# A hybrid recurrent decoder step: dense units moved into the sample steps, masks made a pair ahead, and the RWKV sample steps and norm reordered

## What is computed

```
h = x + 0.5 * swiglu(rmsnorm(x), w_ff1)
P = rmsnorm(h) @ w_in            # one projection: gated DeltaNet, GLA, RWKV-7 and three branch gates
y_A = gated_delta(conv(P_A), state_gdn)      # 6 heads, 128 x 128 state
y_B = gla(P_B, state_gla)                    # 6 heads, 64 x 128 state
y_C = rwkv7(shift(P_C), state_rwkv)          # 12 heads, 64 x 64 state; group norm, bonus, gate
m = sum_i sigmoid(P_gate_i) * (y_i @ w_branch[i]);  h = h + m @ w_out
x = rmsnorm(h + 0.5 * swiglu(rmsnorm(h), w_ff2))
```

## Time and profile before

| | us |
|---|---|
| median of 3 runs (lowest to highest) | 3218.73 (3212.09 to 3221.67) |
| the profiled execution's own time | 3215.23 |
| its span, first to last instruction | 3213.4 |
| PE busy in the span | 3080.0 (96%) |
| DVE, ACT, POOL busy | 1671.0, 1182.4, 109.9 |
| mean granted TensorE clock | 0.974 of full speed |

### The profile page before, as it was taken

The page is one execution under the profiler, slowest core; times in us unless marked ns, Lnnn a source line. Parts: engine busy times, 40 slices in busy tenths (PEclk is TensorE's granted clock), DMA queues, the critical chain, the costliest instruction groups (busy, mean ns, idle before and its releaser), DMA issues.

```text
span 3213.4 us, 61472 instructions
## 1 busy us (share of the span) xinstructions
PE 3080.0 (96%) x24976; PEld 2966.6 (92%) x24976; DVE 1671.0 (52%) x2174; ACT 1182.4 (37%) x1589; POOL 109.9 (3%) x176
## 2 busy tenths in 40 slices
PE   8999999999899999999889998997999999999998
PEld 7999999999899888888888988886999999999998
DVE  5455445454545665555575546456455444445543
ACT  4343333333434532222253224344343333333333
POOL 1000000001000000000000001011000000000001
PEclk9999999999999999998989989989999999999999
DMA  5555555655455533334553336357545655555553
GB/s 166 166 157 169 172 157 164 171 161 171 124 170 149 152 109 95 90 105 117 166 148 95 101 115 184 108 175 252 165 131 161 170 165 170 158 169 157 167 170 112
DMA packets 599915, 482.51 MB, mean 150 GB/s; under 512 B 29010, under 2 KB 545597, under 8 KB 599389
## 3 DMA queue, kind: packets, MB, share of 16 engines
q1 hardware_dynamic: 575760, 428.45, 45.7%
q0 software_dynamic: 8592, 33.16, 3.4%
q10 hardware_dynamic: 15392, 18.43, 1.6%
HBM read 451.82 MB, written 28.10 MB: 149 GB/s over the span
## 4 chain that ended last, share of the span: by engine, by line
PE 85%; DVE 7%; ACT 3%; issue 2%; DMA 2%; ACTq 0%; POOL 0%; DVEq 0%; POOLq 0%
PE ps L392 25%; PE ps L393 24%; PE ps L394 24%; PE ps L1111 2%; DVE lo L749 2%; ACT hi L559 1%; PE ps L1106 1%; PE ps L1392 0%; DMA smA<-in_dt_bias 0%; PE ps L551 0%; PE ps L2308 0%; PE ps L1405 0%; DMA rawsD<-kept 0%; PE ps L1935 0%; DVE raws L773 0%
## 5 line engine op out<-in xcount | busy, mean ns | idle before, releaser
L392 PE MATMUL ps<-xh,hi 128*128 128x288 f32 x4800 | 1456.4, 303 | 45.7 <-ACT kept L630 11.2
L393 PE MATMUL ps<-xl,hi 128*128 128x288 f32 x4800 | 1430.0, 298 | 0.0
L394 PE MATMUL ps<-xh,lo 128*128 128x288 f32 x4800 | 1429.1, 298 | 0.0
L749 DVE TENSOR_TENSOR lo<-raw,hi 128x1024 fp32r<-128x1024 f32 (+1 forms) x820 | 975.1, 1213 | 542.8 <-ACT hi L559 533.2
L559 ACT ACTIVATE hi<-raw 128x1024 fp32r<-128x1024 f32 (+1 forms) x820 | 832.5, 1042 | 843.3 <-PE ps L394 797.6
L392 PEld LDWEIGHTS ps<-xh,hi 128*128 128x128 f32 x4800 | 915.9, 191 | 77.8 <-issue 25.1
L393 PEld LDWEIGHTS ps<-xl,hi 128*128 128x128 f32 x4800 | 916.2, 191 | 0.6
L394 PEld LDWEIGHTS ps<-xh,lo 128*128 128x128 f32 x4800 | 915.8, 191 | 0.0
L393 PE MATMUL ps<-hidl,hi 128*128 128x288 f32 x1376 | 406.9, 296 | 0.0
L392 PE MATMUL ps<-hidh,hi 128*128 128x288 f32 x1376 | 406.9, 296 | 0.0
L394 PE MATMUL ps<-hidh,lo 128*128 128x288 f32 x1376 | 404.3, 294 | 0.0
(11 more groups left out here) (680 smaller groups left out, 2022.0 us busy)
## 6 DMA issues: line engine op xcount, KB each, us to landing
raw<-in_w_ff_up SPq DMA_DIRECT2D x688, 256.0 KB, 4.1
raw<-in_w_in SPq DMA_DIRECT2D x448, 256.0 KB, 3.0
raw<-in_w_ff_down SPq DMA_DIRECT2D x344, 256.0 KB, 3.4
raw<-in_w_out SPq DMA_DIRECT2D x64, 256.0 KB, 3.0
raw<-in_w_branch SPq DMA_DIRECT2D x48, 256.0 KB, 3.0
gatesD<-kept ACTq DMA_DIRECT2D x24, 288.0 KB, 3.0
gates<-gatesD POOLq DMA_DIRECT2D x8, 864.0 KB, 7.2
raw<-in_w_branch SPq DMA_DIRECT2D x48, 128.0 KB, 3.4
```

What stands on the lines that cost most here:

```text
L392: pe.matmul(out, w, rh, start=start, stop=False)
L393: pe.matmul(out, w, rl, start=False, stop=False)
L394: return pe.matmul(out, wl, rh, start=False, stop=stop)
L749: dve.tensor_tensor(lo[:, q, 0:wide], raw[:, q, 0:wide], hi[:, q, 0:wide].bitcast(F32), SUB).then_inc(lo_ready[q], 1)
```

## The change

The number of dense units in all is the same. What changes:

- The table `U`: one unit more in each sample step of RWKV (`ssz`) and A (`asso`), four more in those of GLA (`bsso`), one more behind GLA's chunk steps (`bsco`), fewer before RWKV's norm (`rec`, `fin2`) and more behind it (`fin4`). Behind GLA's head norm 210 dense matmuls stood before; now there are 126.
- RWKV's sample steps: two buffers `sdC`, loaded two pairs ahead; PE transposes the next pair's states right behind the product with 8 columns of this pair; DVE copies only the 64x64 blocks, back into the buffer; the mask is made one pair ahead. The next load now waits until the pair's new states are copied (`C_so8`).
- RWKV's norm: the bonus products are made first, into `rsF`; mean, variance and bonus sums follow one another; gain, bonus, shift and gate are fused into 12 instructions of 288 columns.
- A's start: `rowsA` and `smA` are loaded before `mixer_done`, and `projA` as soon as PE has read `proj` the last time; 36 small copies become 2; ACT copies the old rows out later.
- The waits for the stored prompt state: in A moved down, in B gone (POOL alone waits, between its two loads). GLA's masks are made one pair ahead, and a `presplit(2)` is added in GLA's start.
- In `branch` ACT makes the high half of `merged` one slot later, behind the next split; `out` no longer waits for all groups before it to be read.

```diff
-                if not (down or name.startswith("up") and name != "up00" and name != "up10"):
+                if not (down or name == "out" or name.startswith("up") and name != "up00" and name != "up10"):
                     pe.wait_ge(acc_empty, p["group0"])
...
+            def merged_high(k):
+                act.wait_ge(sem("gated"), k + 1)
+                pair = slice(2 * k, 2 * k + 2)
+                act.activation(xh[:, pair, :], merged[:, pair, :], ACT.Copy).then_inc(sem("merged_hi"), 1)
...
+                            if s % 2 == 0 and it * 4 + s // 2:
+                                merged_high(it * 4 + s // 2 - 1)
...
-                        if name == "branch":
-
-                            act.wait_ge(sem("gated"), it * 4 + (g + 1))
-                            pair = bass.ds((it * 4 + g) * 2, 2)
-                            act.activation(xh[:, pair, :], merged[:, pair, :], ACT.Copy).then_inc(sem("merged_hi"), 1)
+                        if name == "branch" and it * 4 + g == KD // 2 - 1:
+                            merged_high(it * 4 + g)
...
-        U = dict(feat=6, hist=12, shift=60, rec=6, root=3, bfeat=8, lora=6, lora2=3, kk=8, prod=7, tok=2,
-                 wz=2, z=1, scz=1, sco=2, s0t=2, ssz=2, szt=2, sso=3, s8t=2, fin=4,
-                 conv=3, head=8, hl=8, aba=4, gc=6, aprod=7, az=4, ascz=2, asco=6, assz=2, asso=3,
-                 bgk=20, fin2=15, hn=8, afin=6, afin2=8, bfin=2, bfin2=16, bprod=4, bsco=6, bsso=4)
+        U = dict(feat=6, hist=12, shift=60, rec=2, root=3, bfeat=8, lora=6, lora2=3, kk=8, prod=7, tok=2,
+                 wz=2, z=1, scz=1, sco=2, s0t=2, ssz=3, szt=2, sso=3, s8t=2, fin=5,
+                 conv=3, head=8, hl=8, aba=4, gc=6, aprod=7, az=4, ascz=2, asco=6, assz=2, asso=4,
+                 bgk=20, fin2=2, fin3=3, fin4=8, hn=8, afin=6, afin2=8, bfin=2, bfin2=16, bprod=4, bsco=7, bsso=8)
...
+            load_sd(1)
             for p in range(BT):
-                e.need("C_sd_used")
-                if p < BT - 1:
-                    load_sd(p + 1)
                 e.need("C_so8")
+                if p < BT - 2:
+                    load_sd(p + 2)
                 for par in range(2):
                     pool.dma_start(o["rwkv_s"][0, :, 2 * p + par].rearrange("b v k -> v b k"),
...
+                        state_turned(p0)
                         for p in range(3):
-                            e.eng.wait_ge(sem("C_sd"), 32 * (p0 + p + 1))
-                            for k in range(NSEQ):
-                                mm = pe.transpose(ps[:, k // 4, k % 4 * P:k % 4 * P + P], t["sd"][:, k, :], ident[:, :])
-                            e.mark(mm, "C_s0t")
-                            weave(U["s0t"])
...
                             e.mark(mm, "ss_z")
+                            if p < 2:
+                                state_turned(p0 + p + 1)
+                            weave(U["s0t"])
                             e.need("ss_v_kept")
+                            if p:
+                                e.need("C_so8")
                             for k in range(2):
                                 out = ps[:, k, :].rearrange("p (b v) -> p b v", v=P)
                                 pe.matmul(out, t["klT"][0:32, p, :], t["vm"][:, 4 * k:4 * k + 4, :], start=True, stop=False)
...
-                            e.need("C_so8")
+                        e.need("C_so8")
 
             weave(U["rec"])
-            e.need("C_recurred")
             for p in range(BT):
                 mm = pe.matmul(ps[:, p, 0:NT], ones64[:, :], ybuf[:, YC + p, :], start=True, stop=True)
...
-            e.need("hn_sq")
+            e.need("hn_sq", 2)
...
-            e.need("hn_sq")
+            e.need("sums_read", 2)
             for p in range(BT):
-                mm = pe.matmul(ps[:, p, 0:NT], ones64[:, :], sqF[:, p, :], start=True, stop=True)
+                mm = pe.matmul(ps[:, p, 0:NT], ones64[:, :], rsF[:, p, :], start=True, stop=True)
             e.mark(mm, "hn_sum")
-            weave(U["fin"])
+            weave(U["fin3"])
...
-            weave(U["fin"])
+            weave(U["fin4"])
...
+                        state_kept(p0)
+                        masked_v(0)
                         for p in range(3):
-                            e.need("C_s0t")
-                            e.mark(dve.tensor_copy(t["s0"][:, :, :], psf[:, 0:1024].rearrange("p (b v) -> p b v", v=P)), "C_s0_kept")
...
+                            if p < 2:
+                                masked_v(p + 1)
...
             for p in range(BT):
-                e.link(dve.tensor_scalar(Y[:, p, :], Y[:, p, :], par1[:, R_LNW + p:R_LNW + p + 1], par1[:, R_LNB + p:R_LNB + p + 1], MUL, ADD))
-                ins = dve.scalar_tensor_tensor(sqF[:, p, :], proj[:, p, 0:NT], par1[:, R_RK + p:R_RK + p + 1], proj[:, 6 + p, 0:NT], MUL, MUL)
+                ins = dve.scalar_tensor_tensor(rsF[:, p, :], proj[:, p, 0:NT], par1[:, R_RK + p:R_RK + p + 1], proj[:, 6 + p, 0:NT], MUL, MUL)
...
+            weave(U["rec"])
+            e.need("hn_sum", 2)
+            e.link(dve.scalar_tensor_tensor(Y, PS6, -1.0 / 64, Y, MUL, ADD))
+            e.mark(dve.tensor_tensor(sqF[:, :, :], Y, Y, MUL), "hn_sq")
+            dve.wait_ge(sem("C_so8_stored"), 6)
+            dve.nop().then_inc(sem("C_recurred"), 1)
             weave(U["fin"])
+            weave.presplit(2)
...
+            e.mark(dve.tensor_tensor(rsF[:, :, :], PS6, proj[:, 12:18, 0:NT], MUL), "gn_bonus_used")
+            weave(U["fin2"])
+            e.need("fin_rs")
+            e.link(dve.tensor_tensor(Y, Y, sqF[:, :, :], MUL))
+            for p in range(BT):
+                e.link(dve.scalar_tensor_tensor(Y[:, p, :], Y[:, p, :], par1[:, R_LNW + p:R_LNW + p + 1], rsF[:, p, :], MUL, ADD))
+            weave(U["fin3"])
             e.need("hn_sum")
-            e.link(dve.tensor_tensor(Y, PS6, Y, MUL))
+            for p in range(BT):
+                e.link(dve.scalar_tensor_tensor(Y[:, p, :], Y[:, p, :], par1[:, R_LNB + p:R_LNB + p + 1], ps[:, p, 0:NT], ADD, MUL))
+            weave(U["fin4"])
             dve.nop().then_inc(sem("mixer_done"), 1)
...
-            pool.wait_ge(sem("mixer_done"), 1)
             pool.dma_start(rowsA[0:24, :], i["state_gdn_conv"][0].rearrange("b j n -> (b j) n")).then_inc(sem("a_landed"), 16)
+            for k, name in ((0, "a_log"), (1, "dt_bias")):
+                pool.dma_start(smA[:, k, :], i[name][0].partition_broadcast(P)).then_inc(sem("a_landed"), 16)
             pool.wait_ge(sem("kept_stored"), 16 * GROUPS_A)
+            e.need("hn_sum", 5)
             for k in range(4):
                 pool.dma_start(proj[:, 6 * k:6 * k + 6, :], projA[:, 6 * k:6 * k + 6, :]).then_inc(sem("projA_landed"), 16)
...
-            for k, name in ((0, "a_log"), (1, "dt_bias")):
-                pool.dma_start(smA[:, k, :], i[name][0].partition_broadcast(P)).then_inc(sem("a_landed"), 16)
+            state_in = lambda h: i["state_gdn"][0, :, h].rearrange("b k v -> k b v")
+            pool.wait_ge(sem("mixer_done"), 1)
+            load_state(pool, tA[1], 0, "A", state_in, 3)
+            load_state(pool, tA[1], 1, "A", state_in, 3)
...
+            load_state(pool, tA[1], 2, "A", state_in, 3)
...
+            pe.wait_ge(sem("mixer_done"), 1)
...
-            e.need("last_turned")
-            e.mark(act.activation(rowsA[0:27, :], psf[0:27, 512:512 + 2304], ACT.Copy), "rows_kept")
+            e.link(act.activation(spare, ones[:, 0:1], ACT.Silu))
+            e.need("last_kept", 2)
...
+                if m == 1:
+                    e.need("last_turned")
+                    e.mark(act.activation(rowsA[0:27, :], psf[0:27, 512:512 + 2304], ACT.Copy), "rows_kept")
...
+            tails = proj[:, 0:18, SEQW:PW].rearrange("p m (b t) -> p m b t", t=7)
+            e.link(dve.tensor_copy(tails[:, :, :, 0:GAP], ps[:, 0, 0:432].rearrange("p (m b t) -> p m b t", b=NSEQ, t=GAP)))
...
+            e.mark(dve.tensor_copy(lastA[:, :, GAP:27].rearrange("p m (b t) -> p m b t", t=GAP), tails[:, :, :, TS:]), "last_kept")
...
-                    dve.wait_ge(sem("state_stored"), 1)
...
+                if b == 2:
+                    dve.wait_ge(sem("state_stored"), 1)
...
+            load_state(pool, tB[1], 0, "B", state_in, 2)
             pool.wait_ge(sem("out_stored"), 16 * stored)
-            pool.nop().then_inc(sem("state_stored"), 2)
...
+            load_state(pool, tB[1], 1, "B", state_in, 2)
...
+            weave.presplit(2)
...
-                    dve.wait_ge(sem("state_stored"), 2)
...
+                    masked_v(0)
+                    for p in range(3):
...
+                        if p < 2:
+                            masked_v(p + 1)
```

109 lines of the change are left out of this document (52 added, 57 removed).

## The result

| | us |
|---|---|
| after: median of 5 runs (lowest to highest) | 3194.04 (3188.97 to 3200.81) |
| before, beside it on the same chip: median of 5 | 3221.67 (3212.09 to 3228.76) |
| ratio, 95% interval | 0.9911 (0.9889 to 0.9933) |
| the profiled execution of after: own time, span, clock | 3200.81, 3199.0, 0.972 |

The account below looks back on a forecast made before the run. PE is busy 96% of the span, so only its idle time and clock loss can be won; terms sum to 60, less 4 for `kept`, 56 us under the profiled 3215.2, giving 3159, predicted as 3161 us (3148 to 3177).

Parts of the forecast that it names:

- RWKV's sample steps: 0: RWKV's sample steps: idle won 2.2 us, new waits cost 7.6, clock gains 5; sum 0, between -6 and +8.
- two new waits: RWKV's sample steps: PE waits for DVE's state copy, 2.8 us in all, and for the late load, 4.8.
- its clock's term: RWKV's sample steps: a third of the 13.8 us lost to the lower clock comes back, 5 us.
- A's start: Start of A, 1593 to 1640 us: wait for `smA` goes, idle and clock loss shrink; gain 17 us, 8 to 21.
- the 4 for `kept`: PE's waits for `kept` in five places, 9.3 us: groups' ends shift, so 4 us is set against them.
- A's sample steps with GLA's start: A's sample steps gain 5 us by a unit more per step; GLA's start gains 4 by the added presplit.
- branch and out: End of the mixers: branch gains 8.5 us as DVE's wait for ACT's split goes; out gains 4.5, half its loss.
- some 5 where a new wait falls in: RWKV's sample steps: us without a dense unit where a new wait falls, against 4.2 before and 2.7 in other steps.
- RWKV's norm: RWKV's norm, 1550 to 1593 us: bonus products first and fused instructions under dense units gain 5 of 5.8 us.
- A's and GLA's third blocks: Third blocks of A and GLA: the wait behind POOL's store of the prompt state goes, gaining 6.5 and 5.5 us.
- GLA's sample steps: GLA's sample steps, clock 0.61: four more units win back a third of 12.1 us lost, 4 us, 0 to 9.
- the early load starves the weights: Rival, chance 0.2: loading `projA` crowds out weights, A's start gains 9 us, branch 0 to 2; 3177 to 3185 us.

Follow-up runs that it names:

- rwkv_steps_as_before: The kernel after with RWKV's sample steps alone in their old form, dense units per step as in after: 3173.66 us, 0.9857 of before.
- Group 5: Best version of the study (paced gate loads, 49 units moved) with RWKV's steps as in after, 3179.85 us, with either of two edits, or with both, 3164.99 us.
- turned_behind_mask_product: After, with RWKV's next transposes behind the mask's product and its three units, and two units ahead of each half's first product: 3173.94 us, 0.9862; again 3171.39, 0.9869.
- group 5's single edits: RWKV's order of after plus two dense units in each half's first pair, 3172.90 us, or plus transposes moved behind the mask's product, 3172.65 us.
- a_start_as_before: turned_behind_mask_product with A's start alone in its old form (load order, 36 small copies, early copy of old rows): 3184.61 us, 0.9906 of before.
- no_late_loads: After without the loads of RWKV's sample states for pairs 2 to 5, which then work on old data: 3175.67 us, 0.9866 of before.
- the base: turned_behind_mask_product run again unchanged, beside the kernels of the third group: 3171.39 us, 0.9869 of before.
- gates_paced: turned_behind_mask_product with POOL asking for a pair's gates and raws in branch three pairs ahead instead of four: 3169.36 us, 0.9847 of before.

## Why the prediction was wrong

The direction was right, and the gain came to half of the sum: 28.9 us by the stages for 56. The step that failed is "RWKV's sample steps: 0". It took 12 of the missing 27 us. Its two new waits were forecast, somewhat too short; what failed is its clock's term, in which a wait cost its length only and the clock was to gain 5 us. The other 15 are terms whose mechanism was seen and whose size was not: A's start with the prompt blocks behind it (7.9 for 13, the 4 for `kept` taken off), A's sample steps with GLA's start (4.1 for 9), GLA's blocks (6.1 for 9.5), branch and out (10.2 for 13).

- **RWKV's sample steps**, forecast 0 with -6 as its lower end, measured -8 (68.1 left before, 76.3 in the second profile of after's order) to -15 (the profile after, with its two long falls of the clock); by the runs the old order in after's place is 17 us faster.

  Its terms: the waits for the copy 3.1 us for the forecast 2.8; the waits for the load 6.6 for 4.8, because PE's product starts 0.6 us ahead of POOL's issue, not 0.2, and the states are there 4.5 us behind it, not 4.1 (rows below); a third wait of 0.4 us four times, which I had not seen, for the state's sum that DVE now does in two instructions before line 1422. That is 11.1 us of new waits for 7.6.

  The clock's term fell the other way: +5 forecast, 0 to -7 measured. It was computed as if a wait cost its length only. The prediction's own sentence had the cause ("some 5 where a new wait falls in") and gave it no price. Without the late load the clock's loss is 8.6 us in place of 13.8, and the 5 looks right, but by these single profiles that is luck: rwkv_steps_as_before has 9.8 with none of the new order, so most of it may have come with the third dense unit of each step.

  That the waits cost time is shown; what one costs through the clock is known less well. Group 5 took away 10.6 us of waits (11.3 to 0.7) and got 13 us by the ratios, 15 by the medians; between after and turned_behind_mask_product it is 10.4 us of waits and 16 by the ratios. Both differences of ratios are known to 9 or 10 us only, so neither excludes the bare length. In the stage's profiles 14.0 and 21.2 us went with these waits; of group 5's single edits one took 7.5 us with 4.4 us of waits, the other 7.4 with 7.5.

  Timeline of PE and POOL in after, second pair of the first half:

```profile
1435.16 1.85 PE L1394 MATMUL ps<-wrC,sdC 128*128 128x8 f32 x16
1440.35 0.90 PE L1385 MATMUL ps<-ident,sdC 128*128 128x128 f32 x3 [3.35 <-DMA sdC<-in_state_rwkv]
...
1435.80 1.35 POOL L1250 DMA_DIRECT2D sdC<-in_state_rwkv  x2 [50.11 <-DVE so8C L1743]
```

- **RWKV's norm**, 5: measured 4.9 (from line 1418 to 1434 before, 33.5 us with 138 dense; from line 1429 to 1445 after, 17.6 with 60). Right.
- **A's start**, 17, with most of the 4 set against it for `kept`: 12 to 13 when it is undone alone; from before to after 7.1 up to A's first PE row and 0.8 behind it. In its own window the term is right: 13.4 us of idle and 8.5 of clock became 3.4 and none, for the forecast 2.5 and 2.5. The prompt blocks behind it, which the prediction left out, gave 9 us of it back: 10.8 us of idle and 2.3 of clock became 12.7 and 9.2 (1640 to 1870 us), and idle is larger there in every profile of a kernel with the rest of the change, 12.5 to 15.3 us from 30 us behind A's first PE row to block 3, a_start_as_before with its old start among them (14.1). So it isn't the new start that costs it, and no run tells what does. The wait for `smA` is gone, as forecast; the later waits for `kept` are not (8.7 us for 9.3), they sit at other groups' ends. The early load of the projections, which I had in the middle of the mechanism, is worth 0 to 3 by the runs.
- **A's and GLA's third blocks**, 6.5 and 5.5: for A 7.4; for GLA it can't be told apart from the units.
- **A's sample steps and GLA's start**, 9: measured 4.1. The load of `s0A` is still waited for (1.1 us, 1.4 before), one head later, but over the profiles the wait does shrink with the longer step: 1.4 to 2.8 us in the four with before's numbers of units, 0.3 to 2.8 with the change's 26 units more, at most 0.9 with 49. Against the gain stands the wait at the end of A's norm, 3.9 us for 0.7, where DVE stands at ACT's gate; it goes with the number of units, and with 49 moved it is 1.4 and the stage 8 us shorter. That the units shift what ACT does ahead of the gate is my reading, not tested alone. The clock's term wasn't there either: 0.86 for 0.89.
- **GLA's sample steps**, 4, with the blocks 9.5: 6.1, the clock from 0.61 to 0.80 as said.
- **Branch and out**, 13: 10.2, alone 9.7. `out` gave what was forecast. In branch DVE's wait of 1.49 us is gone and the late groups are 5.9 us apart, but two of the early ones are 9.9 and 7.8 us long, where the weights were late. The rival *the early load starves the weights* was right about the place in branch and wrong about A's start.

Of the moved units the prediction said that by themselves they are worth nothing and pay where they cover a wait or keep the clock up. 49 of them gave 8 us, 0.2 us each, in that way. The 26 that the change moved into A and GLA gave 3 us by the medians and none by the ratios when they were taken out again; the terms that lean on them (A's sample steps 5, GLA's 4) had 9.

The rule on transposes that the prediction weighed (the Trainium skill, "TensorE: Matmul & The Clock Gate", "Part 4: PE-mode transpose") leaves the transposes beside the product without effect on the clock; the prediction's terms were 5 us without such an effect and 9 with it. no_late_loads, with transposes right behind the product, has 5.2 us less clock loss than before, and only 1.2 less than rwkv_steps_as_before, which has no transposes there. The trace agrees with the rule, as far as one profile of each can. The rule on queues (the Trainium skill, "DMA: Bandwidth & Descriptors", "Queues, rings and completion order") is that a DMA engine takes turns between queues a whole packet at a time. In branch POOL's queue (`q0`) has packets of 4.2 KB in the mean and the weights' (`q1`) of 0.9 KB, and POOL's has the larger share of the engines' time (after, 2203 to 2222 us):

```profile
q0 software_dynamic: 1099, 4.59, 66.3%
q1 hardware_dynamic: 2495, 2.35, 38.0%
```

The trace agrees with the rule in the direction, and 10.5 us of ACT's waits for weights in the base became 1.0 with the burst cut.

Open stay: why the same instructions leave the clock down for 3.4 us or for 13.6; what one of RWKV's waits costs through the clock; why A's prompt blocks lost what its start had gained; and the true worth of the early load, on which runs and stages differ.

## What to carry to other kernels

A new wait between pieces with no dense work can cost more than its length, since the clock's fall can come with it: here the runs' middle values say 1.2 to 1.5 times, with intervals that don't exclude its bare length. So when work is moved ahead of its data by a few microseconds, place it behind work that is ready in any case: two units later the same transposes still waited 1.7 us, behind the mask's product and three units more they didn't wait at all. And look behind the place that you repair, since A's start gained what was forecast in its own window and the blocks behind it lost half of that. Load bursts should be cut to what the next groups need: here weights came late beside a full queue although the branch's mean rate fitted.

## What the runs showed of the hardware

The clock's return is not a function of the instructions alone: 13.6 us at 0.50 in one execution, 3.4 us in another, over the same matmuls (the windows of group 5). The DMA engines carried the branch's peak (share 1.04, 360 GB/s from 2172 to 2191 us in gates_paced) with 1.0 us of waits for weights and DVE's groups 5.9 us apart, although in after a similar rate (1.05, 366 GB/s from 2203 to 2222) went with 10.6 us of such waits and groups of 9.9 and 7.8; a share near 1 is not by itself a bound. And a single profiled execution misled by 3 us in a stage that nobody had touched.
